# Identity products in the first gates and a new order of the last up slots in a two-block transformer kernel

## Chip, core and metric

The kernel runs on one core of a Trainium2 chip. The metric is the device time of one execution in microseconds. The engines are TensorE (PE; its weight loads are shown apart, as PEld), VectorE (DVE), ScalarE (ACT), GpSimd (POOL) and SyncE (SP), which issues most of the loads.

## What is computed

Two blocks, each of two layers, on a model width of 1024. The part that matters here is the first block: 16 meta tokens and 256 tokens, so 272 columns, and in each layer a latent attention and a retention mixer side by side, then a gated feed-forward part.

```python
for l in range(DEPTH):                      # DEPTH = 2
    h = rms_norm(h_res, attn_norm_g[l])
    z = h @ w_in[l]
    c_q, c_kv, k_pe, rq, rk, rv, rg = jnp.split(z, split_idx, axis=-1)
    y_mla = mla_mixer(c_q, c_kv, k_pe, ...)
    y_ret = retention_mixer(rq, rk, rv, rg, ...)    # silu(rg) * normed retention
    h_res = h_res + jnp.concatenate([y_mla, y_ret], axis=-1) @ w_out[l]
    hf = rms_norm(h_res, ffn_norm_g[l])
    gate, up = jnp.split(hf @ w_gate_up[l], 2, axis=-1)
    h_res = h_res + (jax.nn.silu(gate) * up) @ w_down[l]
```

The second block (a pooling mixer, then a differential attention over 256 latent and 256 context tokens, each with feed-forward parts before and behind, all modulated by products of a condition vector with large weights) follows on the result. All matrices are float32.

## The kernel before

Every activation lies with the model width on the 128 partitions and the tokens in the columns. Each float32 matrix product is made of three products of the faster type: weights and activations are split into a high part (a rounded copy) and a low part (the rest), and hi x hi, hi x lo and lo x hi are summed in PSUM. Weights come in slots of up to 16 tiles of 128 x 128. A slot passes through SyncE's load into `raw[b]`, ScalarE's copy into `w_hi[b]` (line 1461, `split`), VectorE's subtraction into `w_lo[b]` (line 1951, `split`), and TensorE's products; there are two buffers, b = 0 and 1, so a slot's split can start when TensorE has done with the slot two before it, and the next load into `raw[b]` when the low part is made. One program runs per engine, in written order, and semaphores tie them.

**The first gates.** In `layer1` the retention's gate projection is four gemms, `gate(0)` to `gate(3)`, each of eight steps k with three products (lines 938 to 940). Behind each step of `gate(0)` stand thin products, sums over partitions with a vector of ones that give one column: `q_thin` (line 1017) for k = 0 to 3, three sums a step (fewer in layer 1, where the meta tokens' queries are left out), and `k_thin` (line 1025) for k = 4 to 7, three a step. A float32 product shows as two records. Between the halves of gate(0) stands `r_pv(3)` (line 1003), behind it `v_turn(1)` (line 921, 12 transposes), gate(1), the rows of k's norm (line 950) and gate(2) with `r_thin` (line 1033, two a step). `keep_clock(n, bank)` (lines 688 to 692) issues n float32 products of the identity with 272 columns of the table into a PSUM bank that nothing reads; it already stands at the norms.

**The deferred feed-forward parts.** In both layers' feed-forward parts of the first block the norm's row is applied late: TensorE multiplies unnormed activations, and VectorE scales both results (`hidden_scaled`, lines 2133 and 2136: gate, then hidden). Each part has two halves: an up phase (12 slots of 16 tiles, then 10) and a down phase (8 slots of 12 tiles, then of 10). For an up slot the chain is: VectorE's gate scaled into `sg`; ScalarE's silu in place (line 1556); VectorE's hidden scaled into `midf`; `hidden_product` (2141); ScalarE's rounding into `mid_hi` (1563); VectorE's `hidden_lo` into `mid_lo` (2149). The down products take mid_hi and mid_lo; the first down slot waits for the last two of them before its last two tiles. `scaled_slot` orders VectorE as: scaled, low part of the slot before, split of the slot after next, product. `modulation` then runs one turn of the second block's conditioning (`ada`: lines 2103, 2105, 2108, for even slots only here, and none in the last down phase). In the loops both engines run a hardware loop (`Fori`) over all pairs of slots but the last (VectorE writes out the first too). The last pair is written out, and its splits are those of the first two down slots. In layer 1's second half (`ni == CTX_NORM`) the last pair also carries the start of the next norm's context half: `derive(0, 0)` (2570, 2572), `scaled_half` (2031) and `lo_half` (2040) on VectorE, with `norm2_half` (1497) on ScalarE between them; the other six of these follow in the down slots, behind `clear_sum` and `residual`.

## Time and profile before

| | us |
|---|---|
| median of 3 runs (lowest, highest) | 2304.03 (2303.01, 2305.49) |
| the profiled execution | 2302.83 |
| its span, first to last instruction | 2301.2 |
| TensorE busy | 2258.3, 98% of the span |
| VectorE, ScalarE, GpSimd busy | 64%, 37%, 7% |
| mean granted TensorE clock | 0.994 |

The rows from the trace stand further down. Times in them are microseconds from the span's start. The mean granted clock is the share of 2.4 GHz; 0.5 is 1.2 GHz. Matmul records overlap: the spacing of two starts tells the rate, not the duration of one. An idle time in brackets is that of the engine just before the instruction, with what ended it.

### The profile page before, as it was taken

How to read it: one execution, taken by the hardware profiler on the slowest of the kernel's cores; microseconds unless marked ns; L12 is line 12 of the kernel's file. 1: busy time of each engine (PE TensorE's matmuls, PEld its weight loads, DVE VectorE, ACT ScalarE, POOL GpSimd, SP SyncE). 2: the span in 40 equal slices, each digit the busy share in tenths (PEclk: the TensorE clock that was granted, in tenths of full speed). 3: DMA queues.
4: the chain of work that ended last, by engine and by line, in shares of the span. 5: the costliest groups of instructions: out<-in, count | busy, mean ns of one | idle time of the engine just before them, and what ended most of it. 6: DMA issues, size and time to landing. Idle time of an engine off the chain costs nothing.

```text
span 2301.2 us, 37388 instructions
## 1 busy us (share of the span) xinstructions
PE 2258.3 (98%) x14172; PEld 2033.1 (88%) x14172; DVE 1462.8 (64%) x2310; ACT 847.0 (37%) x1130; POOL 160.2 (7%) x235
## 2 busy tenths in 40 slices
PE   8999999999999999999999999999999999999998
PEld 8999999999999988888888888888888888879998
DVE  4547777556778787678778767773333346556555
ACT  4445444435634432222432222232212234445443
POOL 0110000130000110001001101000000001000000
PEclk9999999999999999999999999999999999999999
DMA  6225665323665565455335545433233223123553
GB/s 230 98 74 195 206 239 174 124 83 103 210 237 187 180 207 183 164 192 177 106 130 204 182 162 199 160 115 110 77 105 109 71 95 127 56 74 128 173 192 128
DMA packets 65483, 343.21 MB, mean 149 GB/s; under 512 B 7152, under 2 KB 10480, under 8 KB 42608
## 3 DMA queue, kind: packets, MB, share of 16 engines
q1 hardware_dynamic: 44656, 266.47, 33.3%
q0 software_dynamic: 20736, 75.51, 9.8%
q8 instruction: 59, 0.97, 0.2%
q14 instruction: 32, 0.26, 0.0%
HBM read 340.90 MB, written 1.05 MB: 149 GB/s over the span
## 4 chain that ended last, share of the span: by engine, by line
PE 79%; issue 11%; DVE 6%; ACT 3%; DMA 1%; POOL 0%; DVEq 0%; SPq 0%; ACTq 0%; POOLq 0%
PE gpt L841 20%; PE gpt L843 19%; PE gpt L842 19%; DVE w_lo L1951 2%; ACT w_hi L1461 2%; PE gpt L938 1%; PE gpt L766 1%; PE gpt L939 1%; PE gpt L940 1%; PE gpt L767 1%; PE gpt L768 1%; PE mbt L1121 1%; PE gpt L1336 1%; PE gpt L1337 1%; PE gpt L1338 1%
## 5 line engine op out<-in xcount | busy, mean ns | idle before, releaser
L841 PE MATMUL gpt<-xn_hi,w_hi 128*128 128x512 f32 (+2 forms) x2256 | 747.3, 331 | 5.7 <-DVE w_lo L1951 5.7
L842 PE MATMUL gpt<-xn_lo,w_hi 128*128 128x512 f32 (+2 forms) x2256 | 742.8, 329 | 0.0
L843 PE MATMUL gpt<-xn_hi,w_lo 128*128 128x512 f32 (+2 forms) x2256 | 742.7, 329 | 0.0
L1951 DVE TENSOR_TENSOR w_lo<-raw,w_hi 128x2048 fp32r<-128x2048 f32 (+2 forms) x280 | 567.6, 2027 | 249.7 <-ACT w_hi L1461 249.5
L1461 ACT ACTIVATE w_hi<-raw 128x2048 fp32r<-128x2048 f32 (+2 forms) x280 | 476.4, 1702 | 390.9 <-PE gpt L843 356.5
L841 PEld LDWEIGHTS gpt<-xn_hi,w_hi 128*128 128x128 f32 x2256 | 426.5, 189 | 46.6 <-issue 7.1
L842 PEld LDWEIGHTS gpt<-xn_lo,w_hi 128*128 128x128 f32 x2256 | 426.6, 189 | 37.6
L843 PEld LDWEIGHTS gpt<-xn_hi,w_lo 128*128 128x128 f32 x2256 | 426.5, 189 | 37.5
L841 PE MATMUL gpt<-mid_hi,w_hi 128*128 128x512 f32 (+2 forms) x996 | 333.1, 334 | 4.7 <-DVE mid_lo L2149 4.5
L842 PE MATMUL gpt<-mid_lo,w_hi 128*128 128x512 f32 (+2 forms) x996 | 332.2, 334 | 0.0
L843 PE MATMUL gpt<-mid_hi,w_lo 128*128 128x512 f32 (+2 forms) x996 | 332.2, 334 | 0.0
L1553 ACT ACTIVATE sg<-gpt 128x512 f32<-128x512 f32 (+1 forms) x88 | 47.9, 544 | 548.9 <-PE gpt L843 531.4
L841 PEld LDWEIGHTS gpt<-mid_hi,w_hi 128*128 128x128 f32 x996 | 188.4, 189 | 24.4 <-DVE mid_lo L2149 5.7
L842 PEld LDWEIGHTS gpt<-mid_lo,w_hi 128*128 128x128 f32 x996 | 188.5, 189 | 18.3
L843 PEld LDWEIGHTS gpt<-mid_hi,w_lo 128*128 128x128 f32 x996 | 188.5, 189 | 18.2
L2145 DVE TENSOR_TENSOR midf<-sg,gpt 128x512 f32<-128x512 f32 (+1 forms) x88 | 54.7, 621 | 213.1 <-ACT sg L1553 212.5
L2103 DVE CUSTOM_DVE_ANT_0 sqb<-ada_w,cond 128x1024 f32<-128x1024 f32 x144 | 175.7, 1220 | 4.6
L2105 DVE CUSTOM_DVE_ANT_0 ada_w<-ada_w,cond 128x1024 f32<-128x1024 f32 x144 | 175.7, 1220 | 0.0
L555 POOL DMA_DIRECT2D ada_w<-in_ada x144 | 76.6, 532 | 903.4 <-DVE mods L2108 898.3
L2290 DVE SCALAR_TENSOR_TENSOR R<-gpt,gcol,R 128x256 f32 (+1 forms) x100 | 44.4, 479 | 115.5 <-PE gpt L843 114.3
L1563 ACT ACTIVATE mid_hi<-midf 128x512 f32 (+5 forms) x132 | 68.5, 519 | 117.1 <-DVE midf L2141 104.3
L2149 DVE TENSOR_TENSOR mid_lo<-midf,mid_hi 128x512 f32 (+5 forms) x132 | 73.0, 553 | 2.2 <-ACT mid_hi L1563 2.0
(341 smaller groups left out, 2734.5 us busy)
## 6 DMA issues: line engine op xcount, KB each, us to landing
raw<-in_up_a SPq DMA_DIRECT2D x72, 1024.0 KB, 4.7
ada_w<-in_ada POOLq DMA_DIRECT2D x144, 512.0 KB, 3.5
raw<-in_up_b SPq DMA_DIRECT2D x60, 1024.0 KB, 4.8
raw<-in_down_a SPq DMA_DIRECT2D x48, 768.0 KB, 4.3
raw<-in_down_b SPq DMA_DIRECT2D x48, 640.0 KB, 3.9
raw<-in_win SPq DMA_DIRECT2D x16, 1024.0 KB, 4.8
raw<-in_qkv SPq DMA_DIRECT2D x12, 1024.0 KB, 4.8
raw<-in_wout SPq DMA_DIRECT2D x8, 1024.0 KB, 4.8
```

The source lines that it names most:

```text
L555: nc.gpsimd.dma_start(ada_w[r % 2][:, :], dram["ada"][it + i * n + r]).then_inc(ada_in[r % 2], 16)
L841: mm(o, w_hi[b][:, j, :], hi(k), start=(k == 0), stop=False)
L842: mm(o, w_hi[b][:, j, :], lo(k), start=False, stop=False)
L843: last = mm(o, w_lo[b][:, j, :], hi(k), start=False, stop=(k == kt - 1))
L1461: A(w_hi[b][:, 0:tiles, :], raw[b][:, 0:tiles, :], ACT.Copy).then_inc(hi_ready, 1)
L1553: A(sg[:, b, 0:n], gp[b][0][:, 0:n], ACT.Silu).then_inc(sg_ready, 1)
L1563: A(mid_hi[:, j, 0:n], midf[:, b, 0:n], ACT.Copy).then_inc(mid_h, 1)
L1951: V.tensor_tensor(w_lo[b][:, 0:tiles, :], raw[b][:, 0:tiles, :], w_hi[b][:, 0:tiles, :].bitcast(F32), ALU.subtract).then_inc(lo_ready, 1)
L2103: V.tensor_tensor_reduce(sqb[:, 2:4, :].rearrange("p a n -> p (a n)"), ada_w[b][:, :], cond[:, 0, :], 1.0, 0.0, ALU.mult, ALU.add, macc[:, ...
L2105: V.tensor_tensor_reduce(ada_w[b][:, :], ada_w[b][:, :], cond[:, 1, :], 1.0, 0.0, ALU.mult, ALU.add, macc[:, b, 1:2]).then_inc(ada_sum, 1)
L2145: V.tensor_tensor(midf[:, b, 0:n], sg[:, b, 0:n], gp[b][1][:, 0:n], ALU.mult).then_inc(evac_done, 1)
L2149: V.tensor_tensor(mid_lo[:, j, 0:n], midf[:, b, 0:n], mid_hi[:, j, 0:n].bitcast(F32), ALU.subtract).then_inc(mid_ready, 1)
```

## The change

Three edits. First, `keep_clock(1, mb[2])` is put behind the thin products of steps 1 and 3 of gate(0) and behind those of step 5, in both layers: six identity products in all. Second, ScalarE's loop over the up slots is kept as a hardware loop only where the norm isn't deferred; for the deferred parts it is written out, with the same order (split, silu, rounding). Third, the last pair changes. On ScalarE the second slot's split goes behind its silu and rounding, and the context half's `norm2_half` for both tiles behind everything. On VectorE, after the first slot, the second slot's scaled values, the low part before it, its product and its own low part come first, then its split; derive, the halves and both calls of `modulation` stand behind that.

```diff
@@ k and q sums @@
                         if i == 11:
                             last.then_inc(q_col, 1)
+                    if k % 2 == 1:
+                        keep_clock(1, mb[2])
...
                         if i == 11:
                             last.then_inc(k_col, 1)
+                    if k == KT - 3:
+                        keep_clock(1, mb[2])
...
@@ ScalarE, ffn @@
-                    with act.Fori(0, up - 1) as i:
-                        for b in range(2):
-                            if late is None:
+                    if late is None:
+                        with act.Fori(0, up - 1) as i:
+                            for b in range(2):
                                 silu(p0 + i, i * 2 + b, b)
-                            split(p0 + i + 1, b, SIDE_T)
-                            if late is not None:
+                                split(p0 + i + 1, b, SIDE_T)
+                                round_hidden(p0 + i, i * 2 + b, b)
+                    else:
+                        for i in range(up - 1):
+                            for b in range(2):
+                                split(p0 + i + 1, b, SIDE_T)
                                 silu(p0 + i, i * 2 + b, b)
-                            round_hidden(p0 + i, i * 2 + b, b)
+                                round_hidden(p0 + i, i * 2 + b, b)
                     for b in range(2):
+                        if late is not None and b == 0:
+                            split(p0 + up, b, cnt)
+                        silu(p0 + up - 1, 2 * up - 2 + b, b)
                         if late is None:
-                            silu(p0 + up - 1, 2 * up - 2 + b, b)
-                        split(p0 + up, b, cnt)
-                        if late is not None:
-                            silu(p0 + up - 1, 2 * up - 2 + b, b)
+                            split(p0 + up, b, cnt)
                         round_hidden(p0 + up - 1, 2 * up - 2 + b, b)
-                        if half == 1 and ni == CTX_NORM:
-                            norm2_half(ni, *HALF_MOD[ni], 1, (b,))
+                        if late is not None and b == 1:
+                            split(p0 + up, b, cnt)
+                    if half == 1 and ni == CTX_NORM:
+                        norm2_half(ni, *HALF_MOD[ni], 1, (0, 1))
...
@@ VectorE, ffn @@
                             split(p0 + up, b, cnt)
                             hidden_lo(2 * up - 2 + b, b)
-                        else:
-                            scaled_slot(up - 1, b, cnt)
-                            if b == 1:
-                                hidden_lo(2 * up - 1, 1)
-                        if half == 1 and ni == CTX_NORM:
-                            if b == 0:
-                                dve.wait_ge(cs_row, 1)
-                                derive(0, 0)
-                            scaled_half(ni, 1, b)
-                            lo_half(ni, 1, b)
-                        modulation(2 * half, up - 1, b)
+                            modulation(2 * half, up - 1, b)
+                    if scaled_by is not None:
+                        scaled_slot(up - 1, 0, cnt)
+                        hidden_scaled(p0 + up - 1, 2 * up - 1, 1)
+                        hidden_lo(2 * up - 2, 0)
+                        hidden_product(p0 + up - 1, 2 * up - 1, 1)
+                        hidden_lo(2 * up - 1, 1)
+                        split(p0 + up, 1, cnt)
+                        for b in range(2):
+                            if half == 1 and ni == CTX_NORM:
+                                if b == 0:
+                                    dve.wait_ge(cs_row, 1)
+                                    derive(0, 0)
+                                scaled_half(ni, 1, b)
+                                lo_half(ni, 1, b)
+                            modulation(2 * half, up - 1, b)
```

## Rows read from the trace of the kernel before

**Rows 1.** The page's busy times: engine, busy us, share, instructions.
```profile
PE 2258.3 (98%) x14172; PEld 2033.1 (88%) x14172; DVE 1462.8 (64%) x2310; ACT 847.0 (37%) x1130; POOL 160.2 (7%) x235
```
**Rows 2.** Stretches: us, busy PE, PEld, DVE, ACT, POOL, PEclk, DMA share, GB/s.
```profile
100.00:122.00 22.00, 22.00 (x133) 20.88 (x132) 3.32 (x9) 7.82 (x14) 4.53 (x2) 0.69 0.23 72
116.00:118.00 2.00, 2.00 (x13) 2.00 (x12) 0.05 (x1) 1.58 (x4) 0.95 (x1) 0.62 0.50 66
150.00:166.00 16.00, 16.00 (x100) 14.27 (x99) 7.56 (x27) 5.46 (x17) 3.02 (x3) 0.79 0.03 12
...
484.00:500.00 16.00, 16.00 (x109) 15.52 (x108) 2.03 (x5) 6.13 (x12) 7.20 (x6) 0.79 0.25 92
```
**Rows 3.** TensorE's timeline, layer 1's first up loop: start, duration, line, tiles, idle before.
```profile
586.10 0.38 PE L841 MATMUL gpt<-xn_hi,w_hi 128*128 128x256 f32 x1 [0.44 <-DVE w_lo L1951]
...
598.76 0.38 PE L841 MATMUL gpt<-xn_hi,w_hi 128*128 128x256 f32 x1 [0.44 <-DVE w_lo L1951]
```
**Rows 4.** ScalarE's weight copy by line: table loads, ns least/median/most, first and last.
```profile
L1461 ACT ACT_TABLE_LOAD  x5: 1283/1283/1283, 563.7 to 618.4; - x5
```
**Rows 5.** TensorE's timeline at the four ends of deferred up phases.
```profile
267.32 0.39 PE L841 MATMUL gpt<-mid_hi,w_hi 128*128 128x272 f32 x1 [0.59 <-DVE mid_lo L2149]
...
364.17 0.39 PE L841 MATMUL gpt<-mid_hi,w_hi 128*128 128x272 f32 x1 [0.86 <-DVE mid_lo L2149]
...
640.99 0.38 PE L841 MATMUL gpt<-mid_hi,w_hi 128*128 128x256 f32 x1 [0.75 <-DVE mid_lo L2149]
...
735.71 0.39 PE L841 MATMUL gpt<-mid_hi,w_hi 128*128 128x256 f32 x1 [2.02 <-DVE mid_lo L2149]
```
**Rows 6.** TensorE's timeline at the first norm: three identity products, then the rows.
```profile
10.77 1.62 PE L692 MATMUL mbt<-tab 128*128 128x272 f32 x6
12.23 0.84 PE L684 MATMUL mbt<-tab,rcol 128*128 128x128 f32 x6
```
**Rows 7.** TensorE's timeline in both first gates, and 12 transposes at full clock.
```profile
104.20 2.27 PE L1003 MATMUL gpt<-ret_p,v_ret 128*128 128x272 f32 x6
...
114.26 2.72 PE L921 MATMUL mbt<-tab,zv 128*16 128x128 f32 x12
...
120.11 2.75 PE L950 MATMUL mbt<-tab,rcol 128*128 128x128 f32 x24
...
142.37 1.47 PE L1110 MATMUL mbt<-tab,zk 128*16 128x128 f32 x12
...
485.14 1.27 PE L1003 MATMUL gpt<-ret_p,v_ret 128*128 128x272 f32 x6
486.34 0.40 PE L938 MATMUL gpt<-xn_hi,w_hi 128*128 128x272 f32 x1
...
489.50 0.52 PE L938 MATMUL gpt<-xn_hi,w_hi 128*128 128x272 f32 x1
...
498.05 2.75 PE L950 MATMUL mbt<-tab,rcol 128*128 128x128 f32 x24
```
**Rows 8.** TensorE's timeline: last pair of layer 1's second up phase, first down product.
```profile
718.63 0.28 PE L841 MATMUL gpt<-xn_hi,w_hi 128*128 128x256 f32 x1
...
730.15 0.28 PE L841 MATMUL gpt<-mid_hi,w_hi 128*128 128x256 f32 x1
```
**Rows 9.** VectorE's timeline at the end of layer 1's second up phase.
```profile
727.70 0.17 DVE L2570 SCALAR_TENSOR_TENSOR amul<-mods,vec 128x16 f32<-128x16 f32 x1
...
729.45 1.22 DVE L2103 CUSTOM_DVE_ANT_0 sqb<-ada_w,cond 128x1024 f32<-128x1024 f32 x1
...
731.93 0.41 DVE L2133 TENSOR_TENSOR sg<-gpt,ssum 128x256 f32<-128x256 f32 x1
...
732.93 1.48 DVE L1951 TENSOR_TENSOR w_lo<-raw,w_hi 128x1280 fp32r<-128x1280 f32 x1
...
735.57 0.47 DVE L2031 SCALAR_TENSOR_TENSOR tn<-R,amul,mbt 128x256 f32<-128x256 f32 x1
...
737.96 1.48 DVE L1951 TENSOR_TENSOR w_lo<-raw,w_hi 128x1280 fp32r<-128x1280 f32 x1
```

## The prediction

> **What bounds the kernel now.** I first read the page's busy times: TensorE is busy 98% of the span [rows 1], so there is next to no idle time to win. What can be won on TensorE is its clock, and the few places where it waits. So the second view is the table of stretches with the granted clock, and the third TensorE's timeline and waits at the places that the diff names.
>
> The clock is at 2.4 GHz nearly always and at 1.2 GHz in three places [rows 2]. A share of 0.69 over 22 us is 13.6 us at half clock (22 x (1 - 0.69) x 2), in layer 0's first gate; 0.79 over 16 us is 6.7 us, once at 150 to 166 (layer 0's latent attention) and once in layer 1's first gate. In both gates TensorE is never idle, but what it did before the fall was steps of three wide products with two or three products of one column between them. The change puts identity products of 272 columns there.
>
> The other places are in the up loops of the two feed-forward parts with deferred gain. In layer 1's first up loop TensorE waits for w_lo at the start of each slot [rows 3], and ScalarE loads an activation table of 1283 ns ten times there: five before the weight copy (line 1461, [rows 4]) and five before the silu. The loads come once per turn of the hardware loop, between 563.7 and 618.4 us; the second up loop has none. At the end of each of the four up loops TensorE waits for the last mid_lo [rows 5].
>
> **Part 1, the identity products.** Six are added, three per layer, each a float32 product that shows as two records. Three of them in a row take 12.23 - 10.77 = 1.46 us [rows 6], 0.49 each, all of it on the bounding engine: 6 x 0.49 = +2.9 us. Nothing hides it.
>
> What they can give back, if the clock holds: from the last retention product to the rows after the second gate layer 0 took 120.11 - 104.20 = 15.9 us. At full clock the same work is that product (486.34 - 485.14 = 1.20), four steps at (489.50 - 486.34) / 3 = 1.05, the 12 transposes of v_turn (12 such at full clock took 1.47 to the end of the last; with the overlap of the next I take 1.3) and the second gate, 24 products of 0.12 to 0.125 and a start, 3.1: together 9.8 us [rows 7]. That is -6.1. In layer 1 the clock fell three steps later: 498.05 - 489.50 = 8.55 against 1.05 + 1.3 + 3.1 = 5.45, so -3.1. Sum: -9.2 + 2.9 = **-6.3**. Bounds: +2.9 to +5.8 if the clock falls all the same (the products at half clock cost twice), -6.9 if the products hide some of their weight loads.
>
> Does the clock hold? In layer 1 it held through the q steps, the wide retention product and three k steps, and fell at the fourth (the 0.52 at 489.50 [rows 7]); in layer 0, with more one-column products in the q steps, it fell at 117.5 - 13.6 = 103.9, before the k steps began. The added products break both series of thin steps in the middle. I find it probable that this is enough, not sure. After the added products VectorE and GpSimd have to deliver earlier: k_rcol is wanted only after v_turn and the second gate (4.4 us at full clock), which the chain of one small VectorE operation and one GpSimd power should meet.
>
> A rule speaks against this part. The row first: 12 transposes at 142.37 took 1.47 us at full clock and no fall is seen there [rows 2, 7]; and in layer 0 the clock came back at 117.5 (a share of 0.62 in 116 to 118), right behind v_turn and less than a microsecond of wide products, so the transposes did not keep it away. The Trainium skill (TensorE: Matmul & The Clock Gate, Part 4: PE-mode transpose) says that transposes don't count as activity the same way as products. By that rule v_turn would bring the clock down in both layers whatever stands before it; that is a rival below.
>
> **Part 2, ScalarE's up slots written out.** The order in the loop stays as it is; what goes is the loop, and with it the state in which the table is unknown at its head. The Copy needs no load of its own before or after (the second loop shows it), so nine of the ten loads go, and one stays before the first silu, under the wait for the norm's rows. Two slots of layer 1's first loop take 598.76 - 586.10 = 12.66 us [rows 3], two of the second loop 730.15 - 718.63 = 11.52 us [rows 8], with the same tiles, the same VectorE work and no wait. Four pairs can win: 4 x 1.14 = **-4.6 us**. The first pair's waits come from VectorE's late start and stay. Layer 0 has no loads in its loops: 0. Bounds: 0 (the loads stay) to -5.
>
> **Part 3, the last pair's order.** The last mid_lo is now made before the last split, and everything else of that pair, the modulation above all, goes behind it. I lay it out for layer 1's second half, where most is moved, with t = 0 at the first down product (730.15 [rows 8]) and the last up slot done at +0.2. VectorE is free then. Gate, hidden, low part of the slot before, product, ScalarE's rounding and mid_lo took 735.57 - 731.93 = 3.64 us including a w_lo split of 1.4 [rows 9]; without it 2.2, so mid_lo is there at +2.45, and the wait of 2.02 us [rows 5] goes. But ScalarE's copy of the last down weights now starts at +2.0; taken as a little shorter than VectorE's 1.48 it ends at +3.3, the VectorE split at +4.8, and TensorE, which has finished its first down slot of 30 products x 0.12 = 3.6, waits for it until +5.0. Before, that slot began at +6.0 (735.71 and the last products). Gain 1.0.
>
> Then VectorE does what it did before under the last up slot: derive, the first scaled and low halves, 729.45 - 727.70 = 1.75; the modulation, 731.93 - 729.45 = 2.48; the second halves, the clear, the residual and a scaled half, 737.96 - 735.57 = 2.39; then the split, 1.5. That is +4.8 + 1.75 + 2.48 + 2.39 + 1.6 = +13.0 [rows 9]. TensorE wants it at 5.0 + 3.6 = +8.6, and had it before without a wait at +9.6. So TensorE now idles some 4.4 us, and this place as a whole is **+3.4 us** later. What had covered these 4.2 us of VectorE work was the last up slot of 5.8 us, in which VectorE is now idle.
>
> No idle stretch of that length lies in this trace; the longest here, 2.0 us, left the clock up. I expect a fall. The layer 1 fall of 6.7 us cost 3.1; this one would partly lie in the idle time, so I take half, **+1.6** (bounds 0 and 3.1).
>
> The other three ends have no derive and no halves. By the same chain w_lo takes mid_lo's place almost to the tenth: with 12 tiles and 36 products of 0.12 to 0.125 (4.3 to 4.5 us) the split is ready at about +5.4, where mid_lo had released TensorE at 0.6 to 0.9 us of wait and the last products after it [rows 5]; 0 to +0.2 each. Behind it the modulation of 2.48 us delays the next one or two splits: 0 to +0.7 each, least in layer 0's first half and most where 10 tiles leave a slot of 3.75 us. Together **+1.5** (bounds -1 and +2.5). ScalarE's rounding ahead of its copy delays nobody else, and SyncE's next load, which waits for this w_lo, has a whole slot.
>
> **Sum:** -6.3 - 4.6 + 3.4 + 1.6 + 1.5 = -4.4 us. The profiled execution took 2302.83 us with a span of 2301.2, 1.2 below the median of the runs, 2304.03; I take the difference from the median: **2299.6 us**.
>
> **Rivals.** (a) *The fall at 150 to 166 changes.* It lies behind the first gate and is not touched, but the work now reaches it 5 us earlier. If it is gone, about -3.1, 2296.5; if one more fall appears somewhere after the shifts, +3.1, 2302.7. For it: these falls depend on when thin work comes, and both layers have it. Against: the four times shown lie within 2.7 us. (b) *The idle time in layer 1 is not there*, because ScalarE and VectorE get through the moved work faster or TensorE has other cover: without 3.4 and 1.6, 2294.6. Against it stands VectorE's strict order. (c) *The part does not do what it says: the table loads stay* because the placement of loads does not depend on the loop: +4.6, 2304.2. Against: the second loop, entered with silu's table, has none. (d) *The transposes bring the clock down* in both gates: from v_turn on half clock, about two falls like layer 1's, +6.2, 2305.8. (e) *The slower side: the identity products don't hold the clock.* It decides at the thin steps themselves: if one product in two steps is not enough, both gates run as before and pay for the products. Then the -9.2 goes, and 2299.6 + 9.2 = 2308.8 us.
>
> **How the numbers follow.** About 0.2% (4.6 us) is what a measurement of this kernel can tell from no change. Chances: forecast 0.43 (its own range 2297 to 2302.3); fall at 155 gone 0.12; one more fall 0.16; (b) 0.10; (c) 0.05; (d) 0.05; (e) 0.09. Faster, below 2299.4: not quite half of the forecast, 0.20, the vanished fall 0.12, (b) 0.10 and 0.03 of the rest, 0.45. Slower, above 2308.6: half of (e) and the upper ends of (d) and of the extra fall, 0.09. The rest, 0.46, is within 0.2%. The range goes from 2294.0, below (b), to 2306.5, above (d), and leaves out (e) and the tails.
>
> **What would show it.** Clock 1.0 in both gates, and L1017 and L1025's products followed by two records of L692; no table load inside layer 1's first up loop and pairs of 11.5 us; no wait for mid_lo at the four ends but one for w_lo there; after layer 1's second up loop one idle stretch of 4 us before the third down slot, and a low clock behind it. I am wrong if the clock still falls between 100 and 125 us, if the idle stretch is short, or if new falls stand elsewhere.

## The result and the profile after

The changed kernel takes **2309.16 us** (median of 20 runs, 2304.84 to 2317.83), the kernel before 2303.14 (20 runs, 2297.76 to 2306.67): a ratio of 1.0033, interval 1.0023 to 1.0043. It is slower by about 6 us, where 4.4 us faster was forecast; measured again twice, it was slower by 4.0 and 4.1 us (e9 and e19 below). The profiled execution took 2311.36 us with a span of 2309.7, against 2302.83 and 2301.2 before, so 8.5 us of span are to be found.

The page's busy times answer to [rows 1], and TensorE's share is the same 98%:

```profile
PE 2260.8 (98%) x14184; PEld 2035.3 (88%) x14184; DVE 1463.0 (63%) x2310; ACT 834.9 (36%) x1121; POOL 160.9 (7%) x235
```

Twelve more records on PE are the six identity products. ACT has nine instructions and 12.1 us less: the table loads. The stretches with the granted clock (the last column but two) answer to [rows 2]; the last three rows are places where the kernel before was at 1.00:

```profile
100.00:122.00 22.00, 22.00 (x180) 21.11 (x181) 7.40 (x17) 7.46 (x14) 4.53 (x2) 1.00 0.32 117
150.00:166.00 16.00, 14.88 (x129) 14.49 (x128) 7.54 (x23) 5.79 (x16) 1.95 (x2) 1.00 0.00 1
484.00:500.00 16.00, 16.00 (x136) 15.80 (x135) 5.97 (x12) 5.79 (x12) 6.31 (x6) 1.00 0.35 121
515.00:545.00 30.00, 29.61 (x170) 26.22 (x169) 10.50 (x27) 9.38 (x24) 2.02 (x2) 0.72 0.10 36
740.00:752.00 12.00, 7.82 (x47) 7.81 (x47) 8.12 (x19) 6.14 (x10) 0.00 (x0) 0.72 0.30 109
1165.00:1180.00 15.00, 13.98 (x87) 13.23 (x86) 10.19 (x22) 6.78 (x14) 1.80 (x3) 0.77 0.26 88
```

All three falls of before are gone, and three others stand elsewhere. The one at 515 to 545, in layer 1's latent attention, is 30 x (1 - 0.72) x 2 = 17 us of half clock.

TensorE's timeline where it begins a slot of the down phases answers to [rows 5] (start, duration, line, tiles, idle time before with what ended it; rows of layer 0's first and second, layer 1's first and second down phase):

```profile
260.98 0.39 PE L841 MATMUL gpt<-mid_hi,w_hi 128*128 128x272 f32 x1 [0.77 <-DVE w_lo L1961]
272.79 0.39 PE L841 MATMUL gpt<-mid_hi,w_hi 128*128 128x272 f32 x1 [2.28 <-DVE w_lo L1961]
...
360.81 0.39 PE L841 MATMUL gpt<-mid_hi,w_hi 128*128 128x272 f32 x1 [1.05 <-DVE w_lo L1961]
365.31 0.39 PE L841 MATMUL gpt<-mid_hi,w_hi 128*128 128x272 f32 x1 [0.49 <-DVE w_lo L1961]
...
639.40 0.38 PE L841 MATMUL gpt<-mid_hi,w_hi 128*128 128x256 f32 x1 [0.89 <-DVE w_lo L1961]
...
651.09 0.38 PE L841 MATMUL gpt<-mid_hi,w_hi 128*128 128x256 f32 x1 [2.37 <-DVE w_lo L1961]
...
736.17 0.38 PE L841 MATMUL gpt<-mid_hi,w_hi 128*128 128x256 f32 x1 [1.37 <-DVE w_lo L1961]
...
744.20 0.58 PE L841 MATMUL gpt<-mid_hi,w_hi 128*128 128x256 f32 x1 [4.18 <-DVE w_lo L1961]
```

The waits for mid_lo are gone, as the change has it. Waits for w_lo have taken their place, and behind these come second ones, of 2.28, 2.37 and 4.18 us. The forecast had the last of these. It did not have the first two. Their cause is on VectorE (timeline, end of layer 0's first up phase, line 1961 the weight split, 2113 the first half of a modulation step):

```profile
259.09 1.76 DVE L1961 TENSOR_TENSOR w_lo<-raw,w_hi 128x1536 fp32r<-128x1536 f32 x1 [0.93 <-ACT w_hi L1465]
260.76 1.22 DVE L2113 CUSTOM_DVE_ANT_0 sqb<-ada_w,cond 128x1024 f32<-128x1024 f32 x1
...
267.73 1.23 DVE L2113 CUSTOM_DVE_ANT_0 sqb<-ada_w,cond 128x1024 f32<-128x1024 f32 x1 [2.13 <-DMA ada_w<-in_ada]
...
270.90 1.75 DVE L1961 TENSOR_TENSOR w_lo<-raw,w_hi 128x1536 fp32r<-128x1536 f32 x1
```

and on GpSimd, whose timeline of ada_w loads is first the changed kernel's, then the kernel before's:

```profile
245.25 0.54 POOL L555 DMA_DIRECT2D ada_w<-in_ada  x1 [11.14 <-DVE mods L2118]
264.00 0.54 POOL L555 DMA_DIRECT2D ada_w<-in_ada  x1 [18.21 <-DVE mods L2118]
```

```profile
240.44 0.54 POOL L555 DMA_DIRECT2D ada_w<-in_ada  x1 [11.50 <-DVE mods L2108]
252.10 0.54 POOL L555 DMA_DIRECT2D ada_w<-in_ada  x1 [11.13 <-DVE mods L2108]
263.47 0.54 POOL L555 DMA_DIRECT2D ada_w<-in_ada  x1 [10.83 <-DVE mods L2108]
```

In these phases there is one step a pair, always in the same buffer, and GpSimd issues the next load only when the step before it is done. Before, each load had a pair's time. Now the last step of the up phase is moved behind the second slot's split, the load for the first step of the down phase goes out at 264.00, the step waits until 267.73, and the split at 270.90 that TensorE needs stands behind it. The issue times of the two kernels, 264.00 and 263.47, are to be read from the first down product, which is at 255.53 in the changed kernel and at 262.44 in the kernel before: the load went out 1.0 us behind it and now goes out 8.5 us behind it.

By marks in the two profiles, the 8.5 us come about as follows (down phase: from its first product to the first product of the next phase):

| stretch | before | after | difference |
|---|---|---|---|
| to layer 0's rows behind the gates (line 950) | 120.11 | 115.04 | -5.1 |
| from there to the end of layer 0's attention | | | -1.8 |
| layer 0, first down phase | 37.07 | 40.05 | +3.0 |
| layer 0, second down phase | 46.50 | 47.57 | +1.1 |
| layer 1, gates | 17.33 | 15.52 | -1.8 |
| layer 1, latent attention | 26.70 | 33.84 | +7.1 |
| layer 1, first up phase | 78.83 | 74.30 | -4.5 |
| layer 1, first down phase | 36.33 | 39.27 | +2.9 |
| layer 1, second down phase | 57.85 | 63.82 | +6.0 |
| a fall of the clock at 1169 us | | | +1.6 |

My theory after this: the table loads and the end of layer 1's second up phase are as forecast; the last pair's order also costs the late ada_w load, twice; and the low clock falls in other places in each execution, so that a term taken from one trace of it is not the kernel's. The rival for the first: VectorE's moved work itself, not the load, is late. The rival for the second: the falls of the changed kernel belong to it.

### The profile page after: what moved, and what is told of

It is laid out like the page before. It is cut to its first block, busy times and chain, and to the rows that moved or that the text cites. A ratio compares the mean times of both kernels' runs of the same rounds, so it can differ in the third digit from the quotient of the medians.

```text
span 2309.7 us, 37273 instructions
## 1 busy us (share of the span) xinstructions
PE 2260.8 (98%) x14184; PEld 2035.3 (88%) x14184; DVE 1463.0 (63%) x2310; ACT 834.9 (36%) x1121; POOL 160.9 (7%) x235
## 3 DMA queue, kind: packets, MB, share of 16 engines
HBM read 340.90 MB, written 1.05 MB: 148 GB/s over the span
## 4 chain that ended last, share of the span: by engine, by line
PE 82%; issue 10%; DVE 5%; ACT 2%; DMA 1%; POOL 0%; SPq 0%; DVEq 0%; POOLq 0%; ACTq 0%
PE gpt L841 21%; PE gpt L842 20%; PE gpt L843 20%; DVE w_lo L1961 2%; ACT w_hi L1465 1%; PE gpt L938 1%; PE gpt L766 1%; PE mbt L1125 1%; PE gpt L767 1%; PE gpt L768 1%; PE gpt L940 1%; PE gpt L939 1%; PE mbt L1382 1%; PE gpt L1340 1%; PE gpt L1341 1%
## 5 line engine op out<-in xcount | busy, mean ns | idle before, releaser
L841 PE MATMUL gpt<-mid_hi,w_hi 128*128 128x512 f32 (+2 forms) x996 | 334.7, 336 | 13.9 <-DVE w_lo L1961 13.6
L1567 ACT ACTIVATE mid_hi<-midf 128x512 f32 (+4 forms) x132 | 68.6, 520 | 114.4 <-DVE midf L2151 101.6
```

Of the source, the lines that this page charges most:

```text
L841: mm(o, w_hi[b][:, j, :], hi(k), start=(k == 0), stop=False)
L1567: A(mid_hi[:, j, 0:n], midf[:, b, 0:n], ACT.Copy).then_inc(mid_h, 1)
```

## The experiments

**One part at a time.** e1 is the kernel before with the six products, e2 with ScalarE's loops written out, e3 with the last pair's order on both engines:

```diff
                             last.then_inc(q_col, 1)
+                    if k % 2 == 1:
+                        keep_clock(1, mb[2])
...
                             last.then_inc(k_col, 1)
+                    if k == KT - 3:
+                        keep_clock(1, mb[2])
```

```diff
-                    with act.Fori(0, up - 1) as i:
...
+                        for i in range(up - 1):
+                            for b in range(2):
...
```

```diff
+                        scaled_slot(up - 1, 0, cnt)
+                        hidden_scaled(p0 + up - 1, 2 * up - 1, 1)
+                        hidden_lo(2 * up - 2, 0)
+                        hidden_product(p0 + up - 1, 2 * up - 1, 1)
+                        hidden_lo(2 * up - 1, 1)
+                        split(p0 + up, 1, cnt)
...
```

> The kernel before with the six identity products alone, 2303.1 us before. Theory 1 (the marks of the two profiles): the first gate of layer 0 runs at full clock, its end comes 5.1 us earlier, and the fall at 155 us, worth 1.8 us, goes too; the last pair's order, which lost 13 us in the changed kernel, is not in this kernel. So about 2296.2 us, if no fall of the clock comes anywhere else. Theory 2 (a fall avoided is paid elsewhere): the same gain in the first 170 us, but a new fall in layer 1's latent attention, at 515 to 545 us, as the changed kernel has it, which takes 7.1 us: about 2303.3 us. Rival (the identity products don't hold the clock): 2306, with 100 to 122 us at 0.69.

> The kernel before with ScalarE's up loops written out alone, the last pair in its old order. Theory 1: the five table loads between 563 and 619 us go and with them 4.5 us of the first up phase of layer 1, and nothing else of the changed kernel's losses comes, since these are the last pair's order: 2298.6 us. Rival: part of the 13 us that the ends of the up phases lost come from the written-out loop (code to be fetched, or another place for a wait), and then this kernel is at 2300 to 2306 us with the waits of the down phases' first slots grown. A fall of the clock near 520 us, before the first of these loops of layer 1, would have to come from the 1 or 2 us by which layer 0's loops shift the work.

> The kernel before with the last pair's order on ScalarE and VectorE alone, ScalarE's loop kept. Theory 1: the ends of the four up phases lose what the two profiles differ by, 3.0, 1.1, 2.9 and 6.0 us: 13.0 us, so 2316 us, with VectorE waiting some 2 us for ada_w in the first halves of both layers. Rival: the ends lose nothing by themselves, the difference of the profiles being noise of where the clock stands: 2303 to 2305 us.

Measured against 2304.04 us: e1 2300.87 (ratio 0.9985, 0.9972 to 0.9998), so **-3.2**; e2 2299.42 (0.9975, 0.9965 to 0.9986), **-4.6**; e3 2314.84 (1.0045, 1.0032 to 1.0058), **+10.8**. The loads are worth what the forecast had, the products half of it, and the order much more than it. e3's four down phases took 40.04, 47.63, 40.77 and 63.99 us, so the order makes the losses without the other two parts. The intervals are some 3 us wide to each side. e1 stands between its two theories and fits neither: half the expected gain, and no fall in layer 1's attention.

The ScalarE groups between 560 and 640 us, in the changed kernel, show the one table load that is left:

```profile
L1560 ACT ACT_TABLE_LOAD x1 | 1.3, 1283 | 0.0
```

**The modulation step moved back.** e4 is the changed kernel with that step of the last pair where it was, behind the first slot's product; the rest of the order is the changed one:

```diff
                         scaled_slot(up - 1, 0, cnt)
+                        modulation(2 * half, up - 1, 0)
                         hidden_scaled(p0 + up - 1, 2 * up - 1, 1)
...
-                            modulation(2 * half, up - 1, b)
+                            if b == 1:
+                                modulation(2 * half, up - 1, b)
```

> The changed kernel with one thing moved back: the modulation step of the last pair's first slot again stands right behind that slot's product, so that GpSimd can issue the next ada_w load a slot earlier. Theory 1 (two modulation steps in a row wait for the load between them): VectorE's waits of 2.1 to 2.3 us for ada_w at 268 and 647 us go, and PE's waits of 2.28 us at 272.79 and 2.37 us at 651.09 with them; the second halves, where the step is 2.3 us of VectorE's work and moves from one side of the second slot's split to the other, change by 0 to 2 us each way: 2309.2 - 4.6 = 2304.6 us, range 2302 to 2307. Rival (VectorE's own work in front of the residual is what is late, not the load): no change, 2309 us.

Measured: **2294.63 us** (2292.15 to 2296.33; 0.9957, 0.9944 to 0.9970), 9.4 under the kernel before it and 14.5 under the changed kernel's 20 runs. That is three times what was expected. The down phases took 37.34, 47.46, 36.32 and 58.92 us, 10.7 us less in all than in the changed kernel's first trace; the rest goes with the clock, whose mean is 0.998 in these five runs and 0.994 in those 20. GpSimd's load is back under the up phase (e4, ada_w loads):

```profile
246.16 0.54 POOL L555 DMA_DIRECT2D ada_w<-in_ada  x1 [11.14 <-DVE mods L2118]
257.48 0.54 POOL L555 DMA_DIRECT2D ada_w<-in_ada  x1 [10.77 <-DVE mods L2118]
```

What I had not expected is the gain in layer 1's second down phase, 4.9 us, where no load follows. VectorE's timeline there, first the changed kernel, then e4:

```profile
731.24 0.42 DVE L2143 TENSOR_TENSOR sg<-gpt,ssum 128x256 f32<-128x256 f32 x1 [2.56 <-PE gpt L843]
...
734.55 1.49 DVE L1961 TENSOR_TENSOR w_lo<-raw,w_hi 128x1280 fp32r<-128x1280 f32 x1 [0.74 <-ACT w_hi L1465]
...
737.71 1.22 DVE L2113 CUSTOM_DVE_ANT_0 sqb<-ada_w,cond 128x1024 f32<-128x1024 f32 x1
...
742.58 1.48 DVE L1961 TENSOR_TENSOR w_lo<-raw,w_hi 128x1280 fp32r<-128x1280 f32 x1
```

```profile
718.03 1.22 DVE L2113 CUSTOM_DVE_ANT_0 sqb<-ada_w,cond 128x1024 f32<-128x1024 f32 x1
...
720.68 0.42 DVE L2143 TENSOR_TENSOR sg<-gpt,ssum 128x256 f32<-128x256 f32 x1
...
723.75 1.49 DVE L1961 TENSOR_TENSOR w_lo<-raw,w_hi 128x1280 fp32r<-128x1280 f32 x1 [0.74 <-ACT w_hi L1465]
...
729.30 1.48 DVE L1961 TENSOR_TENSOR w_lo<-raw,w_hi 128x1280 fp32r<-128x1280 f32 x1
```

The step of 2.5 us fills the time in which VectorE waited 2.56 us for the last up slot. From one w_lo to the next it is then 729.30 - 723.75 = 5.55 us, not 742.58 - 734.55 = 8.03, and TensorE waits 1.70 us where it had waited 4.18. These 2.5 us are half of the 4.9; much of the rest goes with the 6.8 us of half clock behind the long wait, which e4's trace doesn't have. TensorE in e4, start of the second and third down slot:

```profile
725.37 0.38 PE L841 MATMUL gpt<-mid_hi,w_hi 128*128 128x256 f32 x1 [1.13 <-DVE w_lo L1961]
...
730.92 0.38 PE L841 MATMUL gpt<-mid_hi,w_hi 128*128 128x256 f32 x1 [1.70 <-DVE w_lo L1961]
```

**Two parts without the order.** e5 is e1 and e2 together, the last pair untouched; e13, e15 and e17 are e5 again.

> The kernel before with the identity products and ScalarE's written-out loops, the last pair in its old order: the change without its third part. Theory 1 (the last pair's order is all of the loss): against the kernel before, the time without any low clock falls by 4.5 us (table loads) and rises by 1.3 us (what the identity products cost when the clock would have stood anyway, from the first of these kernels), and the low clock falls from 32 us a run to some 10 to 20, at 0.38 us each: 2292 to 2296 us, and every end of an up phase as in the kernel before. Rival: the gain of the two parts is not a sum, the falls avoided come back in layer 1's latent attention at 515 to 545 us, as in the changed kernel, and the time is 2298 to 2301 us.

> The kernel with the identity products and the written-out loops, last pair in the old order, once more beside the others: 2295 us within 1.5 us, its four waits for mid_lo at 0.59, 0.85, 0.72 and 2.02 us again, the falls of the clock in other places than in its first trace.

e5 measured 2295.05 us against 2303.86 (0.9959, 0.9946 to 0.9972), e13 2295.33 against 2303.82 (0.9969, 0.9955 to 0.9983). The parts add up: -3.2 and -4.6 make -7.8, measured -8.8 and -8.5. This and e4 are the fastest versions, level with each other and faster than both kernels. The four waits for mid_lo stand in e13 as in [rows 5], at 0.58, 0.86, 0.72 and 2.02 us. So the last pair's order, which was to remove them, gains nothing even where its step is put back: e4 and e5 are 0.4 us apart. They are level for different reasons. e4's four down phases are 2.6 us longer than e5's (37.06, 46.66, 35.85 and 57.82), so the order still costs something, but its five runs have a mean clock of 0.998 where the 13 of e5 and e13 have 0.9963, about 8 us less of half clock. Why its clock is higher, no run shows.

**Load or work?** e8 is the changed kernel with VectorE's order untouched, but the last pair's step reads the second ada_w buffer, so that GpSimd need not wait for it. It did that for the down phases too; e18 does it for the up phases alone (VectorE's part of the edit; GpSimd's loads and the count of the buffers follow it and are left out here):

```diff
                     if n == 1 and b == 0 and count:
-                        ada(it + i, 0, turns[0] + i)
+                        if ends and ph % 2 == 0:
+                            ada(it + i, 1, turns[1])
+                        else:
+                            ada(it + i, 0, turns[0] + i)
```

> The changed kernel with VectorE's order untouched, but the modulation step of each last pair in layers 0 and 1 reads the second ada_w buffer, so that GpSimd issues the load behind it without waiting for that step. Theory 1 (the load is late, not VectorE's work): the waits for ada_w at 268 and 647 us go, and 2.0 to 2.3 us in each of the two first halves with them; the second halves have no load behind them that counts and keep their 1.1 and 6.0 us. So 4 to 5 us under the changed kernel. Rival (the step itself is in the residual's way): under 1 us in each half, within 1.5 us of the changed kernel, VectorE's wait being replaced by its work.

e8 measured 2305.38 us. The wait of 2.28 us was gone, and yet layer 0's first down phase took 39.90 us, and layer 1's 38.48. Waits of 0.66 and 1.03 us had come at the end of layer 0's, with ScalarE waiting up to 4.75 us for weights there; e8 issues two ada_w loads in one go at 278.94. So it left open whether another wait takes the load's place by itself.

> As the run with the load hidden (e8), but the second ada_w buffer is used for the last pairs of the up phases alone, so that no two loads are issued in one go at the end of a down phase. Theory 1 (the load that comes late is the loss, and the later waits of e8 came from its own doubled loads): the first down phases of layers 0 and 1 take 37.3 to 38.0 and 36.6 to 37.3 us (the kernel before 37.07 and 36.33, the changed one 40.05 and 39.27), and no wait over 0.9 us in them: 4 to 5 us under the changed kernel beside it. Rival (VectorE's moved work is the loss, and waits for weights take the load's place by themselves): 39.5 to 40 and 38.5 us again, 1 to 2.5 us under the changed kernel.

> The changed kernel once more beside the run before it: 2306 to 2310 us, layer 0's and layer 1's first down phases at 40.05 and 39.27 us where the clock is full.

e18 measured **2301.93 us** and e19, beside it, 2308.12: 6.2 us less, with a ratio to the kernel before of 0.9998 (0.9985 to 1.0011) against 1.0021 (1.0011 to 1.0032). The first down phases took 37.90 and 37.38 us, 2.15 and 1.9 less than 40.05 and 39.27, with no wait over 0.89. (e19's own took 39.96 and 40.51, the latter with a fall of the clock in it.) The second ones kept theirs (47.76 and 62.86), as they should. In e18 the load for the first step of the down phase goes out at 246.65, ten us ahead of the first down product (256.93), and the next one at 270.40:

```profile
246.65 0.54 POOL L555 DMA_DIRECT2D ada_w<-in_ada  x1 [10.54 <-DVE mods L2119]
270.40 0.54 POOL L555 DMA_DIRECT2D ada_w<-in_ada  x1 [23.21 <-DVE mods L2119]
```

The late load is shown, at 2.0 us a time. What is left in these two phases, 0.8 and 1.05 us, and the 1.1 us of layer 0's second, I put down to VectorE's moved work and the new wait for w_lo. e4, with the work back in its place, still has 0.3 and 0.4 us of it against the kernel e5 and 0.8 us in layer 0's second; no run separates the two further.

**Where the clock falls.** e9 and e19 are the changed kernel again, e10, e14 and e16 the kernel before again, and e11 the changed kernel without its identity products.

> The changed kernel once more, on the same chip as the others, for a second trace of it. Theory 1 (where the clock falls is settled by the run, within a set of weak stretches): the marks agree to 0.2 us wherever the clock agrees, but the falls stand elsewhere: the one at 520.68 to 537.75 us is not there in this trace or is 3.4 or 6.8 us long, and the time is 2305 to 2311 us. Rival (the fall at 520.68 belongs to the changed kernel): it stands at the same place with the same 17 us.

> The kernel before once more, for a second trace of it. Theory 1 (where the clock falls is settled by the run): the fall of 13.65 us at 103.86 us in the first trace is of another length here, some 3 to 14 us, within the first gate of layer 0; the weak place is the same and its price is not. The time is 2298 to 2306 us. Rival (the place is fixed): 103.9 to 117.5 us again.

> The changed kernel without its six identity products, so the written-out loops and the last pair's order alone. Theory 1 (the three parts add up): before 2303.9, minus 4.6 for the loops, plus 12.8 for the order as it stood between the kernel with the first two parts and the changed one: 2312.1 us, 3 to 5 us above the changed kernel, with the first gate of layer 0 low for 3 to 14 us in its trace. Rival (the identity products give nothing here since falls only move): 2308 us, as the changed kernel.

e9 measured 2307.84 us (1.0020, 1.0009 to 1.0030), e11 2311.72 (1.0031, 1.0017 to 1.0046), e10's single execution 2301.05. With e1 and with e5 against e2 that is three values for the products: -3.2, 2295.05 - 2299.42 = -4.4, and 2307.84 - 2311.72 = -3.9. Each is uncertain by 2 to 3 us.

> The kernel before, third trace. If falls come back in layer 1's latent attention only with the identity products, this stretch (w_out's first product to the next part) is at full clock, 26.70 us, and the first gates hold 3 to 14 us of low clock in layer 0 and 0 or 7 in layer 1. If the place has nothing to do with them, a fall of 3 to 17 us there is as likely as with the products, five in eight.

> Identity products and written-out loops, last pair in the old order, third trace. If falls come back in layer 1's latent attention with the products, a fall of 3 to 17 us stands there (28.3 us or more), with a chance of five in eight; both gates at full clock, 16.27 and 15.52 us from the third retention product to the rows.

e16 and e17 had the same expectations as these two; the four executions took 2300.82 (e14), 2297.50 (e16), 2295.52 (e15) and 2294.80 us (e17). All traces side by side; "gates" is from the third retention product (98.85 and 480.72 us in the kernel before) to the rows of line 950, "attention" from w_out's first product to the next part's; low is the time at half clock in it by the trace's record of the granted clock:

| kernel | layer 0 gates, low | layer 1 gates, low | layer 1 attention, low |
|---|---|---|---|
| before, first trace | 21.26, 13.6 | 17.33, 6.8 | 26.70, 0 |
| before, e10 | 16.53, 3.4 | 17.35, 6.8 | 26.70, 0 |
| before, e14 | 18.09, 6.8 | 15.76, 3.4 | 26.70, 0 |
| before, e16 | 14.90, 0 | 14.15, 0 | 28.27, 3.4 |
| e2 | 16.53, 3.4 | 14.15, 0 | 26.71, 0 |
| e3 | 18.06, 6.8 | 14.14, 0 | 26.70, 0 |
| e11 | 18.08, 6.8 | 17.35, 6.8 | 26.71, 0 |
| e1 (with products from here) | 17.86, 3.4 | 15.52, 0 | 26.70, 0 |
| changed, first trace | 16.28, 0 | 15.52, 0 | 33.84, 17.1 |
| changed, e9 and e19 | 16.27, 0 | 15.52, 0 | 28.29 and 28.27, 3.4 |
| e4, e12 and e18 | 16.27, 0 | 15.52, 0 | 26.68 to 26.71, 0 |
| e8 | 16.27, 0 | 15.52, 0 | 28.25, 3.4 |
| e5 | 16.27, 0 | 15.53, 0 | 32.26, 13.7 |
| e13 | 16.28, 0 | 15.52, 0 | 28.26, 3.4 |
| e15 | 16.28, 0 | 15.52, 0 | 29.79, 6.8 |
| e17 | 16.28, 0 | 15.52, 0 | 26.70, 0 |

The stretch of layer 0's gates in e10 and in e16, both the very kernel of [rows 2] with its 0.69, and layer 1's attention in e5 and e9:

```profile
100.00:122.00 22.00, 22.00 (x173) 21.18 (x173) 7.40 (x17) 7.80 (x14) 4.53 (x2) 0.92 0.32 113
```

```profile
100.00:122.00 22.00, 22.00 (x186) 21.33 (x186) 7.55 (x17) 7.51 (x15) 4.53 (x2) 1.00 0.36 121
```

```profile
515.00:545.00 30.00, 30.00 (x191) 26.99 (x190) 10.65 (x29) 9.23 (x25) 2.03 (x2) 0.77 0.10 36
```

```profile
515.00:545.00 30.00, 29.17 (x218) 26.91 (x218) 14.69 (x39) 13.92 (x38) 2.03 (x2) 0.94 0.11 36
```

Three things follow. First, the products' own price is exact, since e16 has both gates at full clock without them, and the changed kernel with them (TensorE's timeline, e16 and then the changed kernel):

```profile
98.90 1.19 PE L1003 MATMUL gpt<-ret_p,v_ret 128*128 128x272 f32 x6
...
109.48 1.47 PE L921 MATMUL mbt<-tab,zv 128*16 128x128 f32 x12
113.80 2.75 PE L950 MATMUL mbt<-tab,rcol 128*128 128x128 f32 x24
```

```profile
98.76 1.19 PE L1003 MATMUL gpt<-ret_p,v_ret 128*128 128x272 f32 x6
...
110.72 1.47 PE L921 MATMUL mbt<-tab,zv 128*16 128x128 f32 x12
115.04 2.75 PE L950 MATMUL mbt<-tab,rcol 128*128 128x128 f32 x24
```

(115.04 - 98.76) - (113.80 - 98.90) = 1.38 us, and 15.52 - 14.15 = 1.37 in layer 1: 2.75 us for six. Second, they do hold the clock: one fall in 24 gates of twelve traces with them, ten falls in 14 gates of seven traces without. Third, what a fall in the gates costs is not 9.5 us, as in the one trace that I had. The excess over 14.90 and 14.15 is 6.4 + 3.2 = 9.5 there, but in the mean of the seven traces 2.7 + 1.6 = 4.3.

Are the falls that are avoided paid for in layer 1's attention? There is a fall there in seven of twelve traces with the products and in one of seven without; and in none of the four in which layer 1's gates had fallen, but in eight of the 15 in which they had not, e16 of the kernel before among them. So it is no property of the changed kernel, which was my rival. That a clean gate makes a fall there likelier fits the counts, but with so few traces it is not shown.

One account doesn't close in the traces. In them the products avoid 4.3 us, pay 2.75, lose 0.1 to e1's fall and 1.8 - 0.2 us in layer 1's attention (means of the excess over 26.70): about nothing. The runs say 3.2 to 4.4 us. The four profiled executions of the kernel before took 2302.83, 2301.05, 2300.82 and 2297.50 us, all below the median of its runs, 2303.9, and e5's four 2296.33, 2294.39, 2295.52 and 2294.80, which is its median.

The granted clock that stands beside every run closes most of it. The 90 runs of the kernel before that stand beside the experiments have a mean clock of 0.9934, its four traces 0.9945, and a straight line through the 90 gives 0.43 us of time for each us of half clock. So the traced executions had about 5 us less of half clock than the runs. For the products, the mean clock rises from 0.9931 to 0.9958 (e1), from 0.9938 in e2 to 0.9963 in e5 and e13, and from 0.9925 in e11 to 0.9952 in e9 and e19: each time about 12 us less of half clock. As an estimate that is 12 x 0.43 = 5.2 us gained and 2.75 paid, 2.4 net, and the runs' 3.2 to 4.4 agree with it within their uncertainty. Where the slower runs have their low clock, no trace shows.

**What the order costs in several traces.** The four down phases, in us, first trace or e5 ahead of the others:

| kernel | layer 0, first | layer 0, second | layer 1, first | layer 1, second |
|---|---|---|---|---|
| before, e10, e14, e16 | 37.07, 37.07, 37.07, 37.36 | 46.50, 46.71, 46.70, 46.75 | 36.33, 36.14, 36.46, 35.97 | 57.85, 59.31, 59.47, 59.44 |
| e5, e13, e15, e17 | 37.06, 37.07, 37.07, 37.08 | 46.66, 46.61, 46.71, 46.65 | 35.85, 35.85, 36.28, 35.86 | 57.82, 57.92, 57.94, 59.35 |
| changed, e9, e19 | 40.05, 41.54, 39.96 | 47.57, 47.95, 47.71 | 39.27, 40.44, 40.51 | 63.82, 62.96, 63.14 |

Between the last two rows, which differ in the order alone, the means differ by 3.4, 1.1, 4.1 and 5.0 us: 13.7, where the runs give 12.8. Two things are in them that the first traces don't show. The late load brings falls of its own: in the five traces that have it (the changed kernel, e3, e9, e11, e19), five of the ten first down phases have a fall of 3.4 us at the end of the wait of 2.2 to 2.6 us, and none of the 30 in the other 15 traces has. And the last column's 57.85 is the kernel before without a fall; its other three traces have one of 3.4 us right behind the wait of 2.02 us [rows 5], and with it 59.3 to 59.5. The stretches, e9 in layer 0's first down phase and e10 in layer 1's second:

```profile
272.00:282.00 10.00, 7.75 (x50) 7.53 (x49) 7.55 (x13) 2.18 (x2) 1.07 (x2) 0.83 0.63 210
```

```profile
732.00:738.00 6.00, 5.58 (x34) 5.58 (x35) 4.31 (x9) 2.51 (x4) 0.00 (x0) 0.72 0.46 142
```

**Identity products in the attention too.** e6 is e5 with five more, in the middle of the third and second query groups' products with V:

```diff
                                       v_ret[0:ks, j, h * P:(h + 1) * P], start=(j == 0), stop=(j == q))
+                        if q and (h == 1 or (q == 1 and L == 0 and h == 3)):
+                            keep_clock(1, mb[1] if q == 1 and L == 0 else mb[2])
```

> The kernel of the run before it in this list, with identity products also in the latent attention: one in the middle of each product of the third and of the second run of queries with V, a second one in layer 0, five in all, 0.45 to 0.49 us each, so 2.3 us of work. Theory 1 (these small products, 16 rows at a time, are what the clock falls on at 150 to 157 us and, in the changed kernel, at 521 to 538 us): no fall in these stretches and 2 to 5 us a run less of low clock, which about pays for the products: within 1.5 us of the run before it, with a smaller spread. Rival (the falls come from elsewhere and move on): 2.3 us slower, with the same low clock.

Measured: 2295.17 us, within 0.2 us of e5, but from 2291.81 to 2308.60: seven runs of twelve at 2291.8 to 2295.3 and five at 2303.4 to 2308.6. Its trace is of one of the latter, and shows no fall at 150 to 157 but a longer one right behind, 24 x (1 - 0.57) x 2 = 20.6 us:

```profile
157.00:181.00 24.00, 24.00 (x127) 24.00 (x127) 7.62 (x19) 6.91 (x15) 0.00 (x0) 0.57 0.12 44
```

Neither theory holds: the clock is higher in most runs (0.997 to 0.999 in the seven, 0.996 to 0.998 in e5) and lower in the rest (0.994 and 0.995). The spread grew, where it was to shrink.

**The step given away.** e12 is e5 with the last step of layer 1's second up phase moved to layer 0's second down phase (the table of steps per pair and phase):

```diff
-        ADA = {0: (0, ((1, 1), (1, 1), (1, 1), (0, 0))), 1: (15, ((1, 1), (1, 1), (1, 1), (0, 0))),
+        ADA = {0: (0, ((1, 1), (1, 1), (1, 1), (1, 0))), 1: (18, ((1, 1), (1, 1), (1, 0), (0, 0))),
...
```

> The kernel with the identity products and the written-out loops, last pair in the old order, and the modulation step of the last pair of layer 1's second up phase given to another place: layer 0's second down phase does three steps more, layer 1's second up phase one less, layer 2's two less. If VectorE's own work is what the end of layer 1's second up phase waits for, PE's idle time of 2.02 us there falls to 0.3 us or less and no other wait grows, as pairs of the down phases leave VectorE idle: 1.7 to 2 us under the same kernel without the move. Rival: another step takes over there (the halves of the norm behind it), or layer 0's second down phase has no room: no change.

Measured: 2295.00 us, no gain over e5's 2295.05. TensorE's wait fell from 2.02 to 0.96 us, and that down phase from 57.82 to 56.70; layer 0's second down phase went from 46.66 to 48.47. It had no room, so VectorE's cover is short there too.

## Why the prediction was wrong

**Identity products (-6.3).** The direction was right and the size wrong. Their price of 2.9 us is 2.75. The gain of 9.2 us was read from the kernel's only trace as if each execution had it; seven traces without the products give 4.3, the runs' clocks about 5, and the runs themselves 3.2 to 4.4 net of the price. The step that failed is the one that takes 120.11 - 104.20 as the cost of the gate [rows 7]: the same kernel also had this place at full clock (e16).

**Table loads (-4.6).** Right: -4.6 (e2), and -4.5 in the changed kernel's trace, where 78.83 us became 74.30.

**End of layer 1's second up phase (+3.4 and +1.6).** Right to the tenth in the idle time. With t = 0 at the first down product (731.04), the second slot began at +5.1 (forecast +5.0), the split stood ready at 742.58 + 1.48 - 731.04 = +13.0 (forecast +13.0), the idle time was 4.18 us (forecast 4.4) and a fall of the clock lay behind it. The place cost 6.0 us in the first trace and 5.1 in e9, against 5.0. Part of that is luck. The +1.6 was priced as a fall that the kernel before doesn't have, since its one trace kept the clock up behind 2.0 us of idle time; three further traces of it have a fall there. Against the mean of its four traces, 59.0, the changed kernel's three (mean 63.3) cost 4.3 us.

**The other three ends (+1.5).** This is the step that failed on the order: 3.0, 1.1 and 2.9, so 7.0 us. The forecast counted the modulation's 2.48 us of VectorE and not what hangs on its end: GpSimd's next load. 4.05 of the 7.0 us are that load (e18), and the rest is 3.0 us, twice the estimate and above its bound of 2.5. Over several traces it is 8.6 us and not 7.0, because of the falls behind the late load. Of a step that is moved, the text had followed VectorE's queue and SyncE's, and passed over GpSimd's.

**Falls elsewhere.** They were a rival of 0.16 with one fall of 3.1 us. Their real part was larger: 7.1 + 1.6 us in the changed kernel's first trace, though only 1.6 in layer 1's attention in e9 and e19. They may be why that profile lies 2 us above the median, and don't give the sign. The sign comes from the order: with the other two parts in both kernels it costs 2307.84 - 2295.05 = 12.8 us, where 6.5 were forecast. Products and loads gave 8.8 where 10.9 were forecast. Together +4.0, as e9 measured, instead of -4.4.

**Rivals.** (a), that the fall at 150 to 166 goes or another one comes, happened both ways: the changed kernel's first trace and e19 have no fall there, e9 has the same 6.8 us, and the fall in layer 1's attention is new. The one at 150 to 166 comes and goes with the execution. (b), no idle time in layer 1, and (c), the loads stay, are refuted. (d), that the transposes bring the clock down, too: 12 transposes at 110.72 took 1.47 us, the stretch stands at 1.00, and in e16 the same holds with no product before them. The rule of the Trainium skill (TensorE: Matmul & The Clock Gate, Part 4: PE-mode transpose), that transposes are not counted like products, changes nothing here. (e), the slower side, was put at 2308.8 us, near the measured time, but for a reason that did not occur. The side on which I was wrong had a case of its own that I didn't see: the ends of the up phases.

## What to carry to other kernels

A step that is moved is also the release of whatever waits for its end. Before putting one later, list every queue that its semaphore feeds, and give each load behind it the time that it had: here 2.5 us of work in another place cost 2 us, twice, through a load of 3.5 us (the page's median from issue to landing), and, with the fall of the clock behind it, 4.9 us where the work left an idle engine for a busy one. And a loss of clock seen in one trace is a sample: take several traces of the same kernel before an edit is priced with it, and compare the granted clocks of the runs as well as their times. Two versions can be level, as e4 and e5 are, because one does less work in its way and the other had more clock.

## What the hardware did that I had not expected

The same program has its low clock in other places from one execution to the next. The gates of layer 0 had 13.6, 3.4, 6.8 and 0 us of it in four traces of the kernel before, with the stretches between them that have no fall agreeing to 0.5 us. And the loss for a fall varies with the work under it: 13.6 us of low clock cost 6.4 us in the gates, 13.7 cost 5.6 in layer 1's attention, and 17.1 cost 7.1.
